# One load ahead on a shared DMA queue: weights before residuals, the first expert's weights earlier, routing ahead of two row tiles

## The reference, cut to what matters

```python
x = x + g1x * mixer_output(gla_hx, ml_hx, gg_x, mo_x, gla_norm_g, ml_norm_g, w_out, x.dtype)
x = x + g2x * hier_moe(modulate(rmsnorm(x, norm2_g), sh2x, sc2x), rg_w, rg_b, re_w, re_b, e_w_in, e_w_out)
```

## Time and profile before

| | |
|---|---|
| runs | 4237.5, 4239.15, 4241.42 us; median 4239.15 |
| the profiled execution | 4239.15 us, of which the span that the trace shows is 4237.5 |
| TensorE busy | 3770.1 us, 89% of the span |
| VectorE, ScalarE, GpSimd busy | 2245.5, 1513.8, 1122.8 us |
| TensorE's mean granted clock | 0.926 of full |
| this stage | 789 to 999 us |

### The profile page before, as it was taken

The page is one execution under the profiler, slowest core; times in us unless marked ns, Lnnn a source line. Parts: engine busy times, 40 slices in busy tenths (PEclk is TensorE's granted clock), DMA queues, the critical chain, the costliest instruction groups (busy, mean ns, idle before and its releaser), DMA issues. The chain is left out here.

```text
span 4237.5 us, 44454 instructions
## 1 busy us (share of the span) xinstructions
PE 3770.1 (89%) x16978; PEld 2977.3 (70%) x16978; DVE 2245.5 (53%) x2583; ACT 1513.8 (36%) x1912; POOL 1122.8 (26%) x597
## 2 busy tenths in 40 slices
PE   4899988495999999669888699999879899999998
PEld 1788877464878778556666467777667678888886
DVE  6468547745888888656434322222236553353345
ACT  3321211244777777434111222222232332232233
POOL 2221210134111111223311112222034344444443
PEclk8899997697999999779987899999889999999999
DMA  4411224646999999723311212111054423323323
GB/s 150 121 43 70 68 86 133 218 134 257 353 400 400 400 399 400 298 82 130 133 62 35 97 43 71 63 68 58 29 184 139 139 94 96 96 94 100 95 88 106
DMA packets 161972, 639.31 MB, mean 151 GB/s; under 512 B 20824, under 2 KB 44217, under 8 KB 145681
## 3 DMA queue, kind: packets, MB, share of 16 engines
q1 hardware_dynamic: 133920, 554.29, 36.5%
q10 hardware_dynamic: 18096, 52.96, 3.2%
q0 software_dynamic: 9792, 29.81, 1.9%
HBM read 533.37 MB, written 103.63 MB: 150 GB/s over the span
## 5 line engine op out<-in xcount | busy, mean ns | idle before, releaser
L3399 POOL TENSOR_TENSOR t_wl<-t_raw,t_wh 128x1024 fp32r<-128x1024 f32 (+1 forms) x176 | 397.5, 2261 | 543.7 <-ACT t_wh L3451 538.9
L99 PE MATMUL m_b<-b_high,m_high 128*128 128x512 f32 x960 | 414.6, 432 | 27.6 <-ACT m_ob L2347 19.1
L100 PE MATMUL m_b<-b_rest,m_high 128*128 128x512 f32 x960 | 393.4, 410 | 0.0
L101 PE MATMUL m_b<-b_high,m_low 128*128 128x512 f32 x960 | 384.5, 401 | 0.0
L2318 POOL TENSOR_TENSOR m_high<-m_raw,m_one 128x1024 fp32r<-128x1024 f32 x60 | 116.8, 1947 | 917.1 <-PE m_b L101 863.2
L99 PE MATMUL t_b<-b_high,t_wh 128*128 128x512 f32 x768 | 302.8, 394 | 17.9 <-POOL t_wl L3399 17.8
L101 PE MATMUL t_b<-b_high,t_wl 128*128 128x512 f32 x768 | 300.7, 392 | 0.0
L100 PE MATMUL t_b<-b_rest,t_wh 128*128 128x512 f32 x768 | 300.7, 392 | 0.0
L3451 ACT ACTIVATE t_wh<-t_raw 128x1024 fp32r<-128x1024 f32 (+1 forms) x176 | 175.6, 998 | 339.9 <-PE t_b L101 287.1
L99 PE MATMUL zs_z<-zs_hs,zs_high 128*128 128x512 f32 (+1 forms) x632 | 240.2, 380 | 27.8 <-POOL zs_hs L277 27.8
L2347 ACT ACTIVATE m_ob<-m_b 128x512 f32<-128x512 f32 x120 | 71.0, 596 | 501.7 <-PE m_b L101 493.5
(11 more groups left out here) (650 smaller groups left out, 8901.3 us busy)
## 6 DMA issues: line engine op xcount, KB each, us to landing
moe_raw<-in_expert_w SPq DMA_DIRECT2D x79, 2048.0 KB, 10.1
ex_raw<-in_expert_w SPq DMA_DIRECT2D x39, 2048.0 KB, 10.5
t_raw<-in_w_ff SPq DMA_DIRECT2D x128, 512.0 KB, 3.5
m_raw<-in_w_ug SPq DMA_DIRECT2D x60, 512.0 KB, 4.4
yrows<-ex_y ACTq DMA_DIRECT2D x38, 512.0 KB, 11.0
zs_raw<-in_ada_w SPq DMA_DIRECT2D x32, 512.0 KB, 3.9
gates<-m_ob SPq DMA_DIRECT2D x32, 512.0 KB, 2.9
me_g<-gates SPq DMA_DIRECT2D x32, 512.0 KB, 3.7
```

Of the source, the lines that this page charges most:

```text
L99: nc.tensor.matmul(out, w[0], x[0], start=first, stop=False)
L100: nc.tensor.matmul(out, w[0], x[1], start=False, stop=False)
L101: return nc.tensor.matmul(out, w[1], x[0], start=False, stop=last)
L3399: self.nc.gpsimd.tensor_tensor(self.wl[u % self.NW][:, 0:m], self.raw[u % 2][:, 0:m], self.wh[u % self.NW][:, 0:m].bitcast(F32), ALU.subtr ...
```

## The change

It has three parts.

1. In SP's loop the weight is loaded five units ahead instead of four (`weight(4)` is issued before the loop), and it is issued before the residual instead of behind it.
2. The two expert tiles are loaded at `u` = 7 in one go, behind a wait on `left`, instead of at `u` = 14 and 15.
3. In TensorE's order behind unit 15, `count` comes before the transposes of row tile 6, and the first `listing` before those of row tile 7; before, both came behind all of them.

```diff
         gates(1)
+        weight(4)
         for u in range(self.NU):
             sp.wait_ge(self.x1_done, u + 1)
             sp.dma_start(R["x1"][u % KD][:, self.half(u // KD)], self.x1[u % self.NT][:]).then_inc(self.x1_out[u % self.NT], 16)
             if u == 0:
                 outs(7)
+            if u + 5 < self.NU:
+                weight(u + 5)
             if u >= 2 and u + 1 < self.NU:
                 residual(u + 1)
-            if u + 4 < self.NU:
-                weight(u + 4)
+            if u == 7:
+                sp.wait_ge(self.left, NCX)
+                for j in range(2):
+                    sp.dma_start(self.raw[j][:], A["expert_w"][j]).then_inc(self.raw_in[j], 16)
             if u >= 12:
                 rows(u - 12)
-            if u >= 14:
-                sp.dma_start(self.raw[u - 14][:], A["expert_w"][u - 14]).then_inc(self.raw_in[u - 14], 16)
...
         rows(4)
         rows(5)
+        count()
         rows(6)
+        listing(0)
         rows(7)
-        count()
-        listing(0)
         listing(1)
```

## The result

The changed kernel takes 4262.29 us (median of 5 runs, 4255.6 to 4271.98), the kernel before 4239.15 (median of 5, 4235.01 to 4241.93). The ratio is 1.0055, with a 95% interval of 1.0039 to 1.0072: slower by 17 to 31 us. The forecast was 4254, with a range of 4240 to 4268. The profiled execution of the changed kernel took 4256.27 us (span 4254.6), 17 over that of before.

A forecast was written before the change was run, and what follows sets the result against it. TensorE was taken to set the pace in units 5 to 15, with the residual becoming the bound after the change; 18.5 - 4.9 + 1.5 + 2.0 - 2.2 = +14.9 us on 4239.15 gave 4254.0, range 4240 to 4268.

The forecast's parts named there:

- The wait: SP's queue: from its store SP stands at the weight until GpSimd's low(u+3) ends, 5.46 us after x1(u) starts.
- X(4): The start of VectorE's addition x1(4); X(u) is the start of x1(u) in unit u.
- The period of 9.65: Time between x1 starts in the loop: 5.46 + 0.45 + 3.75 = 9.65 us, against 6.74 before; the residual becomes the bound.
- the nine: The periods between x1 starts from unit 2 to unit 11: 68.3 us before, 86.9 forecast, cost 18.5 us (12.7 to 26.2).
- Given back, 4.9: From x1(11) to x1(15), with no weight left and TensorE ahead: 24.3 us instead of 29.2, 4.9 us regained.
- The expert tiles, 2 us: Tiles issued at u = 7: 4096 KB on the queue delay the residual of unit 9, cost 2 us (0 to 3).
- The clock, 1.5 us: TensorE at 1.2 GHz after idling, uncovered only behind x1(11): cost 1.5 us (0 to 5).
- The tail, a gain of 2.2: Behind unit 15: GpSimd's later additions let VectorE's first mark and small scaling run faster, gain 2.2 us (0 to 3.8).
- the clock as the bound: Rival: gaps keep TensorE at 1.2 GHz throughout, its period doubles to 13.5 us; +48 us, 4287; chance 0.05.
- The late loads: Rival: loads were late before unit 3, so earlier ones save up to 6.0 us plus the tail's 3.8; 4229.3; chance 0.03.
- The hidden wait: Rival: SP's wait is hidden and TensorE keeps the pace, period under 7.6 us; 4237, no change; chance 0.12.

The follow-up runs named there:

- res_first: Changed kernel with the residual issued before the weight five units ahead; 4242.52 us against 4241.93 for the kernel before, ratio 1.0003.
- p1: Kernel before with only the weight loads changed (five units ahead, before the residual); 4257.36 us against 4241.93, ratio 1.0034.
- again: The changed kernel unaltered, a second set of five runs; 4259.33 us against 4239.07 for the kernel before, ratio 1.0051.
- p2: Kernel before with only the two expert tiles moved to u = 7; 4240.97 us against 4241.93, ratio 0.9999.
- p3: Kernel before with only TensorE's order behind unit 15 changed; 4243.26 us against 4241.93, ratio 1.0006.
- one_gather: Kernel before with TensorE's order as changed and the second gather moved behind the barrier; 4239.52 us against 4241.38, ratio 0.9997.
- fill: Kernel before with expert tiles at u = 7, and VectorE doing part of the block owners while awaiting the second list; 4241.81 us against 4241.38, ratio 1.0001.
- wait_only: Kernel before with one added SP wait for the split ahead of the residual, transfers unchanged; 4242.53 us against 4239.07, ratio 1.0009.

## Why the prediction was right

The forecast was slower, by 14.9 us, through SP's wait for the split with the residual behind it. Measured was +17.1 in the profiled execution, +18.1 at the barrier, and +23.1 and +20.3 by the medians. Step by step:

- *The wait.* SP's wait for the split, 4.7 us in most cycles (49.6 us in eleven times), is in its rows, and the weight is issued 5.46 us after X(4), as worked out. Shown by `res_first`, which removes it from the residual's way and loses nothing that can be told, and by `p1`, which has it alone.
- *The period of 9.65.* In steady cycles it was 9.56 to 9.86; the residual landed 3.6 to 3.8 us after its issue (forecast 3.75). In `p1` the nine took 17.9 us more, where the forecast said 18.5.
- *Given back, 4.9.* It was 4.6.
- *The expert tiles, 2 us.* The forecast's own steps give 1.1 to 1.9, rounded up. Measured it was more: the period behind them was 12.68, 3.1 over the steady 9.6, and the nine took 3.7 us more than in `p1`; in `again` that period was 14.93. That they cost nothing where TensorE sets the pace (`p2`) I had not worked out. The rule of the Trainium skill that the forecast weighed, descriptors of one ring taken in order ("DMA: Bandwidth & Descriptors", section "Queues, rings and completion order"), fits the residual that landed after 7.3 us instead of 3.8.
- *The clock, 1.5 us.* It was 1.6 in `p1`'s profile and 0 in the changed kernel's.
- *The tail, a gain of 2.2.* This step failed. VectorE did end 2.3 us sooner, and by the mechanism named. But the prediction followed only the first gather, and took its 5 us more as covered by ScalarE's rounding behind the barrier. The barrier itself waits: it opened 1.2 us after the landing of the second gather, some 8 us after the first one's issue. In place of -2.2 it was +1.1 after the parts together and +1.5 in `p3`. Shown by `one_gather`.

Of the rivals, the clock as the bound did not come about: six of the nine periods ran at a granted clock of 1.00. The late loads were none: TensorE's wait before unit 3 is 6.03 us in the changed kernel too, and still VectorE ends it. The hidden wait would have needed periods under 7.6 us.

The forecast of X(15) less X(2) was 17.1 us more than before, and 17.0 were measured. That this is so close is in part luck: the nine periods were 0.6 us cheaper, the expert tiles 1.7 dearer, 0.3 less came back, and the clock took nothing of its 1.5. The tail's 3.3 us are the rest of the way to +18.1. What is between that and the +23.1 of the first five runs is not explained by the stage's rows of that profile. Eighteen us lie within both intervals, the second set gave 20.3, and its own profile has 20.6 in the stage; it stays open whether anything is left.

## What to carry to other kernels

In a queue that issues in order, a load made "one step earlier" than its buffer comes free turns into a wait, and the price is that of the most urgent transfer behind it, here a small residual needed once in a unit. Put what is needed next before what may wait: that swap alone took the loss away. Work out the new cycle from the end of the wait to the landing, and compare it with the pace of the engine that bounds the stage; below that pace it is free, as the wait alone nearly was, and each further tenth of a microsecond is paid in every cycle. And where a stage ends in a barrier, follow each engine's last issue to its landing, every one of them and not only the first; two gathers of a GpSimd that looked idle held it here.

## What the runs showed of the hardware

- Where a gather held the barrier, the work behind it began 5.3 to 5.5 us after the gather's issue (`one_gather`, `fill`), though the profile shows only 1 us busy for it, and 1.2 to 1.3 us after its landing; with two in a row it was 7.8 to 8.1 us from the first one's issue (changed, `again`, `p3`, `res_first`).
- A 256 KB residual landed after 2.5 us with nothing issued for 4.7 us before it (`wait_only`), after 3.6 to 3.8 with 512 KB just in front, and after 7.3 with 4096 KB and a weight in front (changed).
- With waits of 0.6 to 2.7 us in periods of 9.6 us and more, TensorE's granted clock stayed at 1.00 in most and fell in some: it was 1.00 behind a wait of 2.70 us (at 905.53), 0.73 in the period with a wait of 2.57 (at 924.54) and 0.82 in that with 1.88 (at 937.37). The length of the wait alone thus does not tell; what does stays open. In a later stage the clock had been low after one gap of 3.03 us.
- A VectorE instruction on 128x1024 took 3.16 us beside GpSimd's additions and 1.23 clear of them, a scaling of 128x32 2.10 and 0.18 (before, changed).
